# Expert weight places, routing order and token-ordered high and low rows in a transformer kernel

## The chip, the cores and the metric

The kernel runs on one core of a Trainium2 chip. The metric is the time of one execution in device microseconds, as the median of several runs.

## The reference, cut to what matters

A token batch of 256 rows of 1024 floats goes through two blocks of two layers each. The change touches only the mixture of experts in the two layers of the first block:

```python
def grouped_moe(h, router_w, router_bias, w_gate, w_up, w_down):
    xt = h.reshape(B * T, D)                      # T = 256 tokens, D = 1024
    aff = jax.nn.sigmoid((xt @ router_w).astype(jnp.float32))
    biased = aff + router_bias                    # 16 experts in 4 groups of 4
    # the group with the largest sum of its best two, then the best two experts in it
    gates = ...                                   # aff of the chosen two, divided by their sum
    hg = jnp.einsum('nd,edf->nef', xt, w_gate)    # 16 x 1024 x 512
    hu = jnp.einsum('nd,edf->nef', xt, w_up)      # 16 x 1024 x 512
    act = jax.nn.silu(hg) * hu * gates[:, :, None]
    return jnp.einsum('nef,efd->nd', act, w_down) # 16 x 512 x 1024
```

Ahead of it stand an attention mixer and a layer norm, behind it a second layer norm. All is fp32.

## The kernel before

Five instruction streams, one for each engine and one for SyncE (SP), are written by hand and meet through semaphores. `plan()` fixes beforehand in which PSUM bank each result lies (`job`) and in which SBUF slot of 8 KB per partition each piece of weights lies (`load`). SP issues the loads strictly in the order of the plan, each of 1 MB, and waits before each until the earlier user of the slot is done. A layer has 96 such loads for its experts, 12 for each of 8 pairs of experts (4 of gate, 4 of up, 4 of down). There are 18 slots: 0 to 5 are a ring, which also holds the mixer's weights and the output projection's (the last four, `wo0` to `wo3`); 6 to 11 are free once the output projection is done (`y11`); 12 to 17 lie under the attention's buffers and are free after the last head (`O15`). The list `places` says which slot each load takes: six of the ring, six of 12 to 17, six of 6 to 11, and again. In steady state a load goes to the slot of the load 18 before it.

The stages of a layer around the change are these.

- Norm, `norm` on VectorE (DVE) with `norm_and_transposed` on ScalarE (ACT): two tiles of 128 tokens (t = 0, 1), each `bn_stats`, the square root on ACT (`std_of`), and the writing of `x_tok`. TensorE (PE) transposes `x_tok` (L1802), ACT copies the transposes to `xT`, and PE multiplies them by the router's weights (L1807).
- High and low rows. The gather of tokens is a matmul with fp32r operands, so `x_tok` is split into `tok_high` (a copy rounded to fp32r, ACT) and `tok_low` (the rest, DVE, L1319). Both are written in a permuted order by `grouped`: expert weights are loaded with four consecutive rows of the matrix on one partition, so chunk c of 128 features holds every fourth one. ACT and DVE read `x_tok` through `spread`, with a step of four floats, and write consecutive floats.
- Routing, `route` on DVE: from `aff` (the sigmoid, ACT L903) to `chosen`, `gates`, `rank` (after four small products on PE) and `onehot` (L1304), a one-hot matrix of tokens by slots, 64 slots for each expert. `onehot` comes in two parts, for the first 4 experts and for the other 12, and each raises `slots_ready`.
- Gather, `tokens(j, n)` on PE (L1846): for four experts at a time, four results G{j}0 to G{j}3, each of two halves, each half the sum of four matmuls (high and low of both token tiles), with 128 columns of `tok_high` or `tok_low` stationary and 256 columns of `onehot` moving. ACT copies them to `xe`. j = 0 comes ahead of pair 0, j = 1 to 3 within pairs 1, 3 and 5.
- Pair p on PE: 64 matmuls of gate and up in four quarters (L1825), each quarter waiting for its two loads and freeing two slots behind it (`quarter_used`, `Hg`, `Hu`); the scatter of pair p-1 (L1857, L1858) from `y_high` and `y_low`; transposes of the hidden rows; 32 matmuls of down (L1835) into Y0 and Y1. DVE adds the scatter's results to `res` (L1327).
- `overflow`: rounds for experts with more than 64 tokens. The number of rounds is read from `rounds` into a register (L521) on each engine. With these inputs none is run.

## Time and profile before

| | |
|---|---|
| median of 3 runs | 1476.04 us (1474.61 to 1476.43) |
| the profiled execution | 1473.91 us |
| its span, first to last instruction | 1472.1 us |
| PE busy | 1340.2 us, 91% |
| DVE, ACT busy | 730.3 us, 522.2 us |
| expert stage of layer 0, from the first gate matmul to the last down matmul | 174.4 to 382.2 us |
| expert stage of layer 1 | 556.7 to 765.0 us |

The two expert stages are 28% of the span. The profile is of one execution; times in it are microseconds from the start of the span. 1.8 us of the profiled execution lie outside its span. PE's share of busy time is an average; between the norm and the first gate matmul PE is mostly idle, and within the expert stage it is nearly always busy.

### The profile page before, as it was taken

To read this page: it belongs to the slowest core of one execution; us is meant where nothing else is said; L and a number is where in the kernel's file an instruction comes from. 1 tells how busy PE (TensorE), PEld (TensorE's weight loads), DVE (VectorE), ACT (ScalarE), POOL (GpSimd) and SP (SyncE) were. 2 spreads that over 40 slices of the span, in tenths; PEclk is the share of its full clock that TensorE was granted. 3 is DMA by queue.
4 is the path that set the end of the run, shared out by engine and by line. 5 is a ranking of instruction groups with operands and counts; after the bars stand their busy time and mean duration, and the time that the engine had idled before them with its cause. 6 is when DMAs were issued, how large, how long until landed. Compare 5 with 4: busy or idle time off the path is not lost.

```text
span 1472.1 us, 19934 instructions
## 1 busy us (share of the span) xinstructions
PE 1340.2 (91%) x7792; PEld 964.1 (65%) x7792; DVE 730.3 (50%) x1387; ACT 522.2 (35%) x945; POOL 120.8 (8%) x135
## 2 busy tenths in 40 slices
PE   6999699998799879999978899789999888899997
PEld 3867543443376664444437888379998685699985
DVE  0656411211426661211125588587785636477766
ACT  1354321211123531211214323246654445276553
POOL 1012000000000300000002153030000002000000
PEclk9999799999899979999997999899999999999999
DMA  7252899999715288999996526755665440455740
GB/s 235 97 216 100 352 422 421 420 421 421 250 58 203 87 365 343 421 421 421 419 392 214 166 87 104 159 185 187 210 224 194 148 141 1 143 171 173 254 173 29
DMA packets 128050, 347.73 MB, mean 236 GB/s; under 512 B 8208, under 2 KB 84262, under 8 KB 103396
## 3 DMA queue, kind: packets, MB, share of 16 engines
q1 hardware_dynamic: 122576, 330.19, 59.7%
q0 software_dynamic: 4528, 15.84, 4.5%
q8 instruction: 53, 0.87, 0.2%
q10 hardware_dynamic: 868, 0.63, 0.2%
q14 instruction: 25, 0.20, 0.0%
HBM read 342.44 MB, written 4.19 MB: 235 GB/s over the span
## 4 chain that ended last, share of the span: by engine, by line
PE 82%; DVE 8%; DMA 4%; ACT 2%; issue 2%; POOL 0%; SPq 0%; DVEq 0%; ACTq 0%
PE bank L1825 14%; PE bank L1598 13%; PE bank L1964 8%; PE bank L1965 8%; PE bank L1966 8%; PE bank L1835 7%; DMA slot<-in_w_up 3%; PE bank L2085 2%; PE bank L1846 2%; PE bank L2089 2%; PE bank L2087 2%; PE bank L1999 2%; DVE ln_stats L1123 1%; DVE res L1128 1%; PE bank L1631 1%
## 5 line engine op out<-in xcount | busy, mean ns | idle before, releaser
L1964 PE MATMUL bank<-x_high,w_high 128*128 128x256 f32 x912 | 261.8, 287 | 0.0
L1965 PE MATMUL bank<-x_low,w_high 128*128 128x256 f32 x912 | 260.9, 286 | 0.0
L1966 PE MATMUL bank<-x_high,w_low 128*128 128x256 f32 x912 | 260.8, 286 | 0.0
L766 ACT ACTIVATE w_high<-slot 128x1024 fp32r<-128x1024 f32 x190 | 191.1, 1051 | 186.5 <-PE bank L1966 91.1
L1825 PE MATMUL bank<-slot,arena 128*64 128x512 f32 x1024 | 224.2, 593 | 11.8 <-DMA slot<-in_w_up 5.3
L1964 PEld LDWEIGHTS bank<-x_high,w_high 128*128 128x128 f32 x912 | 177.9, 195 | 1.8 <-issue 1.6
L1825 PEld LDWEIGHTS bank<-slot,arena 128*64 128x64 f32 x1024 | 76.2, 137 | 156.4 <-issue 156.4
L1965 PEld LDWEIGHTS bank<-x_low,w_high 128*128 128x128 f32 x912 | 177.8, 195 | 0.0
L1966 PEld LDWEIGHTS bank<-x_high,w_low 128*128 128x128 f32 x912 | 177.8, 195 | 0.0
L766 ACT ACTIVATE arena<-bank 128x512 f32<-128x512 f32 (+9 forms) x120 | 63.8, 540 | 226.1 <-PE bank L1882 86.7
L1495 DVE TENSOR_TENSOR w_low<-slot,w_high 128x1024 fp32r<-128x1024 f32 x88 | 103.8, 1222 | 59.8 <-ACT w_high L766 59.3
L1333 DVE TENSOR_TENSOR arena<-arena,bank 128x512 f32<-128x512 f32 x16 | 11.0, 689 | 216.8 <-PE bank L1825 216.8
L1835 PE MATMUL bank<-slot,arena 128*64 128x512 f32 x512 | 113.4, 596 | 1.1
L1341 DVE SCALAR_TENSOR_TENSOR y_low<-bank,slot_gates,y_high 128x512 fp32r<-128x512 f32 x32 | 24.0, 751 | 139.2 <-ACT y_high L925 138.4
L1598 PE MATMUL bank<-xT,slot 128*128 128x256 f32 x384 | 84.8, 381 | 0.0
L1598 PE MATMUL bank<-slot,arena 128*128 128x512 f32 (+1 forms) x192 | 80.5, 579 | 2.0 <-ACT arena L766 1.1
L1598 PEld LDWEIGHTS bank<-xT,slot 128*128 128x128 f32 x384 | 72.6, 190 | 11.6 <-issue 2.1
L1835 PEld LDWEIGHTS bank<-slot,arena 128*64 128x64 f32 x512 | 35.4, 137 | 66.2 <-issue 63.8
L1504 DVE TENSOR_TENSOR w_low<-slot,w_high 128x1024 fp32r<-128x1024 f32 x44 | 51.9, 1222 | 43.0 <-ACT w_high L766 42.8
L911 ACT ACTIVATE arena<-bank 128x512 f32<-128x512 f32 x16 | 9.6, 597 | 162.1 <-PE bank L1825 162.1
L1598 PEld LDWEIGHTS bank<-slot,arena 128*128 128x128 f32 x192 | 37.0, 195 | 42.9 <-issue 37.0
L693 POOL TENSOR_TENSOR arena<-arena,rinv 128x256 f32<-128x256 f32 (+1 forms) x48 | 38.6, 825 | 248.6 <-DVE rinv L1153 248.3
(284 smaller groups left out, 2070.4 us busy)
## 6 DMA issues: line engine op xcount, KB each, us to landing
slot<-in_w_gate SPq DMA_DIRECT2D x64, 1024.0 KB, 20.7
slot<-in_w_up SPq DMA_DIRECT2D x64, 1024.0 KB, 19.6
slot<-in_w_down SPq DMA_DIRECT2D x64, 1024.0 KB, 21.0
slot<-in_ffn_w_in SPq DMA_DIRECT2D x44, 1024.0 KB, 7.5
slot<-in_ffn_w_out SPq DMA_DIRECT2D x22, 1024.0 KB, 5.1
slot<-in_hgrn_w_in SPq DMA_DIRECT2D x16, 1024.0 KB, 6.8
slot<-in_w_in SPq DMA_DIRECT2D x10, 1024.0 KB, 8.8
slot<-in_w_o SPq DMA_DIRECT2D x8, 1024.0 KB, 5.0
```

The costliest lines, as they stand in the source:

```text
L693: ins = nc.gpsimd.tensor_tensor(w, w, by, ALU.mult)
L766: return nc.scalar.activation(dst, src, ACT.Copy)
L1495: V.tensor_tensor(w_low[c][:, ab, :, :], raw[:, :, P * c:P * (c + 1)], w_high[c][:, ab, :, :].bitcast(F32), ALU.subtract)\
L1504: V.tensor_tensor(flat(w_low[i % 2])[:, half], raw[:, half], flat(w_high[i % 2])[:, half].bitcast(F32), ALU.subtract).then_inc(sem("split" ...
L1598: last = mm(dst, lhs(c), rhs(c), start=(c == 0), stop=(c == n - 1))
L1825: last = mm(banks_gu["gu".index(m)][rows, :], xe[:, 4 * half + c, rows], ws[e][:, c, :], start=(half == 0 and c == 0), stop=(half == 1 and ...
L1835: last = mm(out[rows, :], B["actT"][:, c, rows], slot(W[(l, f"w{e}{c // 2}{names}")], 2, 1024)[:, c % 2, 512 * h:512 * (h + 1)], start=(c ...
L1846: last = mm(b[:, T * i:T * (i + 1)], x[:, t, tok(2 * n + i)], onehot[:, t, 4 * CAP * j:4 * CAP * (j + 1)], start=(k == 0), stop=(k == len( ...
L1964: mm(dst, high[:, k, :], x_high[:, k, :], start=(k == 0), stop=False)
L1965: mm(dst, high[:, k, :], x_low[:, k, :], start=False, stop=False)
L1966: last = mm(dst, low[:, k, :], x_high[:, k, :], start=False, stop=(k == KD - 1))
L1999: last = mm(b[:, tok(h)], k[:, 4 * s + h, tok(t)], q[:, 4 * s + h, tok(t)], start=True, stop=True)
```

## The change

1. `places` has a new pattern of 18: four of the ring, slots 12 to 17, two of the ring, slots 6 to 11. The last six loads of a layer lie in 12 to 17, as before.
2. ACT copies the second transposed half of token tile 0 before it takes the root for tile 1; it evaluates a sigmoid of one column right behind that root; it writes `tok_high` of tile 0 ahead of the router's sigmoid and of tile 1 behind it.
3. DVE writes `tok_low` of tile 0 behind `gates` and of tile 1 between the two parts of `onehot`, no longer ahead of the routing.
4. `tok_high` and `tok_low` are in token order, `grouped` is gone. ACT and DVE read and write consecutive floats, and PE's stationary operand is read through `spread`, 128 columns with a step of four floats (16 bytes). This holds for all 128 gather matmuls of a layer.
5. The first gather uses banks 0, 1, 5, 6 in place of 0, 1, 0, 1, and runs 12 matmuls that need no low rows of tile 1, then 4 with them, then the second halves. Pair p waits for G0 and G1 before its first quarter and for G2 and G3 before its third.
6. Down: the last two chunks are done by halves, so that Y0 is complete eight matmuls before Y1.
7. DVE reads `rounds` into a register before the last pair's additions.

ACT, layer 0, from the first root of the norm to the copies of the first gather (`arena<-bank`), before:

```order
L792 ACT_TABLE_LOAD
L792 ACTIVATE ln_std<-ln_mv,eps 128x1
L766 ACTIVATE xT<-bank 128x4x128
L792 ACTIVATE ln_std<-ln_mv,eps 128x1
L766 ACTIVATE xT<-bank 128x4x128 x3
L766 ACTIVATE tok_high<-x_tok 128x1024 x2
L903 ACT_TABLE_LOAD
L903 ACTIVATE aff<-bank 128x32
L766 ACTIVATE arena<-bank 128x512 x4
```

and after:

```order
L790 ACT_TABLE_LOAD
L790 ACTIVATE ln_std<-ln_mv,eps 128x1
L764 ACTIVATE xT<-bank 128x4x128 x2
L790 ACTIVATE ln_std<-ln_mv,eps 128x1
L809 ACT_TABLE_LOAD
L809 ACTIVATE loaded_table<-eps 128x1
L764 ACTIVATE xT<-bank 128x4x128 x2
L764 ACTIVATE tok_high<-x_tok 128x1024
L905 ACTIVATE aff<-bank 128x32
L764 ACTIVATE tok_high<-x_tok 128x1024
L764 ACTIVATE arena<-bank 128x512 x4
```

The table load and one of the two copies to `tok_high` stand ahead of the sigmoid `aff`, the other copy behind it.

DVE, layer 0, from the gates to the scaling of `res`, before:

```order
L1297 TENSOR_TENSOR gates<-gates,wsum 128x32 [waits dve_chain]
L1300 SCALAR_TENSOR_TENSOR rank<-bank1,chosen 128x32 [waits bank_full1,gates_ready]
L1301 TENSOR_REDUCE most<-bank1 128x1 [waits dve_chain]
L1304 TENSOR_TENSOR onehot<-rank,pos 128x256 x2
L1304 TENSOR_TENSOR onehot<-rank,pos 128x768 x2
```

and after:

```order
L1305 TENSOR_TENSOR gates<-gates,wsum 128x32 [waits dve_chain]
L1264 TENSOR_TENSOR tok_low<-x_tok,tok_high 128x1024 [waits tok_high,gates_ready]
L1309 SCALAR_TENSOR_TENSOR rank<-bank1,chosen 128x32 [waits bank_full1]
L1310 TENSOR_REDUCE most<-bank1 128x1 [waits dve_chain]
L1313 TENSOR_TENSOR onehot<-rank,pos 128x256 x2
L1264 TENSOR_TENSOR tok_low<-x_tok,tok_high 128x1024 [waits tok_high]
L1313 TENSOR_TENSOR onehot<-rank,pos 128x768 x2
```

Before, both `tok_low` stood directly ahead of the first step of the routing (`biased`), and each now follows where the row shows it.

DVE, layer 0, end of the last pair, before:

```order
L1327 TENSOR_TENSOR res<-res,bank5 128x512 [waits bank_full5]
L1327 TENSOR_TENSOR res<-res,bank6 128x512 [waits bank_full6]
L1327 TENSOR_TENSOR res<-res,bank3 128x512 [waits bank_full3]
L521 TENSOR_LOAD rounds [waits bank_free3,bank_free6,rounds_ready,bank_free5,bank_free7]
L521 ISA x2
L1350 COMPARE_AND_BRANCH
```

and after:

```order
L519 TENSOR_LOAD rounds [waits rounds_ready]
L519 ISA x2
L1332 TENSOR_TENSOR res<-res,bank7 128x512 [waits bank_full7]
L1332 TENSOR_TENSOR res<-res,bank5 128x512 [waits bank_full5]
L1332 TENSOR_TENSOR res<-res,bank6 128x512 [waits bank_full6]
L1332 TENSOR_TENSOR res<-res,bank3 128x512 [waits bank_full3]
L1356 COMPARE_AND_BRANCH [waits bank_free6,bank_free3,bank_free5,bank_free7]
```

The reading of the register stands ahead of the four additions instead of behind them.

The diff, cut to its lines with one line around each (lines that only hold "..." stand for what is left out):

```diff
         quarters = [(m, i) for i in range(2) for m in "gu"]
-        blocks = [(None, NSLOT, RAW_SLOTS)[n % 3] for n in range(12 * PAIRS // RAW_SLOTS - 1)] + [NSLOT]
-        places = [b if b is None else b + i for b in blocks for i in range(RAW_SLOTS)]
+        scratch, late = list(range(NSLOT, NSLOT + EXTRA)), list(range(RAW_SLOTS, NSLOT))
+        rounds = 12 * PAIRS // (NSLOT + EXTRA)
+        places = (4 * [None] + scratch + 2 * [None] + late) * rounds + scratch
...
         for n in range(4):
-            job(l, f"G0{n}", bank=n % 2)
+            job(l, f"G0{n}", bank=(0, 1, 5, 6)[n])
...
         eps = sb("eps", [P, 2])
+        loaded_table = sb("loaded_table", [P, 1])
...
             return tokens[:, t, :].rearrange("p (h q c) -> p h c q", h=2, c=4)
-        def grouped(tokens, t):
-            return tokens[:, t, :].rearrange("p (h c q) -> p h c q", h=2, c=4)
...
+            def high_rows(t):
+                copy(tok_high[:, t, :], x_tok[:, t, :]).then_inc(sem("tok_high"), 1)
...
                 half(0, 0)
+                half(0, 1)
                 std_of(2 * l, 1)
-                half(0, 1)
+                nc.scalar.activation(loaded_table[:, :], eps[:, 0:1], ACT.Sigmoid)
...
                 half(1, 1)
-                for t in range(NT):
-                    copy(grouped(tok_high, t), spread(x_tok, t)).then_inc(sem("tok_high"), 1)
+                act.wait_ge(sem("ln_done"), 4 * l + 2)
+                high_rows(0)
...
                 drained(nc.scalar.activation(aff[:, :, :], b[:, 0:NT * E].rearrange("p (t e) -> p t e", t=NT), ACT.Sigmoid), (l, "logit"))
+                high_rows(1)
...
+            def low_rows_of_tokens(l, t):
+                dve.wait_ge(sem("tok_high"), NT * l + t + 1)
+                V.tensor_tensor(tok_low[:, t, :], x_tok[:, t, :], tok_high[:, t, :].bitcast(F32), ALU.subtract).then_inc(sem("tok_low"), 1)
...
                 dve.wait_ge(sem("gates_ready"), l + 1)
+                low_rows_of_tokens(l, 0)
...
                     last.then_inc(sem("slots_ready"), 1)
+                    if first == 0:
+                        low_rows_of_tokens(l, 1)
...
                 link(V.tensor_scalar(res[:, :, :], x_tok[:, :, :], ALPHA, None, ALU.mult))
-            def low_rows_of_tokens(l):
-                for t in range(NT):
-                    dve.wait_ge(sem("tok_high"), NT * l + t + 1)
-                    V.tensor_tensor(grouped(tok_low, t), spread(x_tok, t), grouped(tok_high, t).bitcast(F32), ALU.subtract).then_inc(sem("tok_low"), 1)
...
                         drained(V.scalar_tensor_tensor(y_low[:, c], b[:, :], slot_gates[:, p:p + 1], y_high[:, c].bitcast(F32), ALU.mult, ALU.subtract), (l, f"Y{g}{p}"))
+                n_rounds = more_rounds(dve, l)
...
                         evacuated(dve, (l, f"M{t}{h}{PAIRS - 1}"))
-            def overflow(l):
-                n_rounds = more_rounds(dve, l)
+                return n_rounds
+            def overflow(l, n_rounds):
...
                 norm(2 * l, l, "y", True)
-                low_rows_of_tokens(l)
                 route(l)
-                experts(l)
-                overflow(l)
+                overflow(l, experts(l))
...
-            def down(l, outs, c, names):
-                for h, out in enumerate(outs):
+            def down(l, outs, c, names, halves=(0, 1)):
+                for h in halves:
+                    out = outs[h]
...
                         for k, (x, t) in enumerate(parts):
-                            last = mm(b[:, T * i:T * (i + 1)], x[:, t, tok(2 * n + i)], onehot[:, t, 4 * CAP * j:4 * CAP * (j + 1)],
+                            last = mm(b[:, T * i:T * (i + 1)], spread(x, t)[:, (2 * n + i) // 4, (2 * n + i) % 4, :], onehot[:, t, 4 * CAP * j:4 * CAP * (j + 1)],
...
                     done(last, (l, f"G{j}{n}"))
+                def first_tokens():
+                    bs = [reuse(pe, (l, f"G0{n}")) for n in range(4)]
+                    def parts(n, i, some):
+                        for x, t in some:
+                            last = mm(bs[n][:, T * i:T * (i + 1)], spread(x, t)[:, (2 * n + i) // 4, (2 * n + i) % 4, :], onehot[:, t, 0:4 * CAP],
+                                      start=(x is tok_high and t == 0), stop=(x is tok_low and t == 1))
+                        return last
+                    pe.wait_ge(sem("tok_high"), NT * (l + 1))
+                    pe.wait_ge(sem("tok_low"), NT * l + 1)
+                    pe.wait_ge(sem("slots_ready"), 2 * l + 1)
+                    begin, end = [(tok_high, 0), (tok_low, 0), (tok_high, 1)], [(tok_low, 1)]
+                    for n in range(4):
+                        parts(n, 0, begin)
+                    pe.wait_ge(sem("tok_low"), NT * (l + 1))
+                    for n in range(4):
+                        parts(n, 0, end)
+                    for n in range(4):
+                        done(parts(n, 1, begin + end), (l, f"G0{n}"))
...
                     if p % 2 == 0:
-                        for n in range(4):
+                        for n in range(2):
...
                             done(last, (l, ("Hg", "Hu")[q - 2] + str(p)))
+                        if q == 1 and p % 2 == 0:
+                            for n in range(2, 4):
+                                evacuated(pe, (l, f"G{p // 2}{n}"))
...
                     bs = [reuse(pe, (l, f"Y{h}{p}")) for h in range(2)]
-                    for c in range(MF):
-                        if c % 2 == 0:
-                            for e in range(2):
-                                loaded(pe, (l, f"w{e}{c // 2}{names}"))
+                    for e in range(2):
+                        loaded(pe, (l, f"w{e}0{names}"))
+                    for c in range(2):
                         for h, last in down(l, bs, c, names):
-                            if c == MF - 1:
-                                done(last, (l, f"Y{h}{p}"))
-                        if c == 1:
-                            last.then_inc(sem("rows_used"), 1)
-                pe.wait_ge(sem("tok_low"), NT * (l + 1))
-                pe.wait_ge(sem("slots_ready"), 2 * l + 1)
-                for n in range(4):
-                    tokens(0, n)
+                            pass
+                    last.then_inc(sem("rows_used"), 1)
+                    for e in range(2):
+                        loaded(pe, (l, f"w{e}1{names}"))
+                    for half in range(2):
+                        for c in range(2, MF):
+                            for h, last in down(l, bs, c, names, [half]):
+                                pass
+                        done(last, (l, f"Y{half}{p}"))
+                first_tokens()
...
                 scatter(PAIRS - 1)
```

## Rows read from the trace of the kernel before

**Rows 1.** The chain in order of time, layer 0, 154 to 175: start, us, what

```profile
154.33 1.91 ACT tok_high L766
...
156.27 3.48 DVE tok_low L1319 x2
...
160.07 0.20 DVE biased L1264
...
166.57 1.28 issue
167.85 5.57 PE bank L1846 x32
...
173.45 0.61 ACT arena L766
174.06 0.30 issue
```

**Rows 2.** Timelines, start, us, engine, line, operation [idle]: router to rank, both layers

```profile
153.72 3.18 PE L1807 MATMUL bank<-router,xT 128*128 128x16 f32 x16
...
158.17 1.28 ACT L903 ACT_TABLE_LOAD   x1
159.47 0.20 ACT L903 ACTIVATE aff<-bank 128x32 f32<-128x32 f32 x1
...
166.69 0.19 DVE L1300 SCALAR_TENSOR_TENSOR rank<-bank,chosen 128x32 f32<-128x32 f32 x1 [1.67 <-PE bank L1598]
...
535.91 3.60 PE L1807 MATMUL bank<-router,xT 128*128 128x16 f32 x16
...
542.45 0.20 DVE L1264 TENSOR_TENSOR biased<-aff,rbias 128x32 f32<-128x32 f32 x1
```

**Rows 3.** Groups by line and shape, 100 to 400: count, busy us, mean ns, idle

```profile
L766 ACT ACTIVATE w_high<-slot 128x1024 fp32r<-128x1024 f32 x4 | 4.2, 1060 | 7.6 <-PE bank L1659 7.6
L766 ACT ACTIVATE tok_high<-x_tok 128x1024 fp32r<-128x1024 f32 x2 | 3.9, 2014 | 0.0
...
L1166 DVE TENSOR_TENSOR w_low<-slot,w_high 128x1024 fp32r<-128x1024 f32 x4 | 4.9, 1226 | 7.6 <-ACT w_high L766 7.6
L1319 DVE TENSOR_TENSOR tok_low<-x_tok,tok_high 128x1024 fp32r<-128x1024 f32 x2 | 3.9, 1974 | 3.3 <-ACT tok_high L766 3.3
```

**Rows 4.** The chain at the second gather, in pair 1

```profile
213.86 3.78 PE bank L1846 x32
```

**Rows 5.** Stretches: busy us by engine, granted clock (1.00 is full), DMA share, GB/s

```profile
154.00:156.00 2.00, 2.00 (x13) 2.00 (x12) 0.00 (x0) 2.00 (x2) 0.00 (x0) 0.55 1.04 434
...
170.00:178.00 8.00, 7.05 (x42) 4.81 (x43) 1.27 (x2) 3.62 (x5) 0.00 (x0) 0.92 0.42 175
...
190.00:340.00 150.00, 149.65 (x759) 65.22 (x760) 24.72 (x37) 26.62 (x54) 1.12 (x2) 1.00 1.01 421
```

**Rows 6.** SP's queue of loads: start, us, operation

```profile
133.98 5.77 SPq L630 DMA_DIRECT2D slot<-in_w_gate  x2
...
178.04 0.81 SPq L630 DMA_DIRECT2D slot<-in_w_up  x2
```

**Rows 7.** PE's waits, 174.3 to 382.3: total us, times, longest

```profile
PE bank L1825 <- DMA slot<-in_w_up: 2.6, 2, 1.3
PE bank L1825 <- DMA slot<-in_w_gate: 2.2, 2, 1.3
```

**Rows 8.** End of the last pair, layer 0; L521: ns min/median/max, both layers

```profile
375.10 7.09 PE L1835 MATMUL bank<-slot,arena 128*64 128x512 f32 x32
...
381.43 1.49 ACT L925 ACTIVATE y_high<-bank,slot_gates 128x512 fp32r<-128x512 f32 x2 [5.68 <-PE bank L1835]
...
387.91 0.69 DVE L1123 BATCH_NORM_STATS2 ln_stats<-res 128x6 f32<-128x512 f32 x1 [1.37 <-issue]
...
L521 ACTq TENSOR_LOAD <-rounds x2: 290/383/476, 382.2 to 765.0; - x2
...
L521 DVEq TENSOR_LOAD <-rounds x2: 324/440/557, 386.8 to 769.6; - x2
```

## The prediction

> **What bounds the kernel now.** I read the chain of waits first, in order of time, and looked for where an expert stage starts and what holds it. The reader sees one path there: the copies to `tok_high` on ACT, the two `tok_low` on DVE, the routing on DVE from `biased`, 1.28 us of issue, the first gather of 5.57 us, ACT's last copy and another 0.30 us, and then the first gate matmul at 174.36 [rows 1]. So the high and low rows stand in the path of the routing, though the routing needs nothing of them. Next came the timelines of ACT and PE at that place: the router's products on PE are over at 153.72 + 3.18 = 156.90, but ACT takes the sigmoid at 159.47, behind its two copies and a table load of 1.28 us [rows 2].
>
> Then the DMA. SP can refill a slot only when PE has used it; the first such load of layer 0 goes out at 178.04 [rows 6]. Before that the queues run dry: 42% of 170 to 178 is 3.4 us, so the first 18 loads are in at about 173.4. From 190 on the stage moves 421 GB/s without a gap [rows 5]. 78 loads of 1.049 MB and 2.1 MB of norm rows at 421 GB/s are 199.3 us, from 178.04 to 377.3. PE's last 32 down matmuls run from 375.10 to 382.2 [rows 8], and the second half of them, from about 378.6, needs the last weights. PE itself has only 4.8 us of waits for weights in the whole stage, all in pair 7 [rows 7]. So both the transfers and PE's work hang on the moment when pair 0 starts; the transfers bind, and PE is 4.8 us behind them. Layer 1's stage takes as long, 208.3 us against 207.8.
>
> **The change part by part.** Sums go against the profiled execution (1473.91 us, span 1472.1) and are then taken off the median, 1476.04, which is 2.1 us above it.
>
> *Routing ahead of the high and low rows.* ACT: the table load moves into the idle time ahead of the last two transposes' copies, `tok_high` of tile 0 becomes a copy from consecutive to consecutive floats. Such a copy of 128x1024 is there: 1060 ns for `w_high`, against 2014 ns now [rows 3]. It starts at 154.33 and is done at 155.4, before the router's 156.90. The sigmoid (0.20 us [rows 2]) then follows the router, and `biased` starts at about 157.15, not 160.07 [rows 1]: 2.9 us. In layer 1 the router ends at 535.91 + 3.60 = 539.51 and `biased` can start at 539.75, not 542.45 [rows 2]: 2.7 us. What was removed from this path is queued again where nothing is late: `tok_high` of tile 1 (1.06 us) runs on ACT beside 5 us of routing; `tok_low` of tile 0 takes 1226 ns, as `w_low` does [rows 3], in the 1.67 us in which DVE waits for PE's rank products [rows 2]. `tok_low` of tile 1 stands behind the first part of `onehot` and is ready about 1.3 us after the gather starts; 12 of its 32 matmuls, at 5.57/32 us each or more [rows 1], are 2.1 us, so the gather does not wait. The second part of `onehot` is 1.2 us later and is used in pair 0's last third. These come out at nothing; without the cover, `tok_low` would cost 1.2 us in each layer.
>
> The clock: PE's was at 0.55 of full in 154 to 156 and comes back late in the first gather [rows 5]. PE now does tile 0's router products 1.2 us earlier and idles later, so the clock may fall up to 1.2 us sooner; work in that time would take twice as long. Bounds 0 and 0.6 us in layer 0, none in layer 1, where it has fallen by then; I take 0.3.
>
> *The first gather's banks.* The last matmul ends at 173.42 and the first gate matmul starts at 174.36, after the copy of G3 and 0.30 us [rows 1]. Afterwards G0 to G3 are complete 4 matmuls apart (0.47 us at full clock), pair 0 needs G0 and G1 alone, and their copies (0.61 us each) end 0.2 us before the gather does. Pair 0 starts 0.1 us behind it: 0.8 us in each layer.
>
> *Places of the loads.* Six loads go out behind `O15`, near 126, and no longer behind 133.98 and the output projection's weights [rows 6]. The first 18 loads are in at about 163 instead of 173.4. That alone gains nothing, since the refill starts with pair 0. It sees to it that a pair 0 that starts earlier finds its weights and that the queues are free. In steady state every load still follows the one 18 before it. The last six now follow the ones 14 before, not 12, with the queues still full then: nothing.
>
> *Down by halves.* Y0 is ready some 0.9 us sooner, ACT's two `y_high` (1.49 us back to back [rows 8]) are no longer back to back, and Y1's can start 0.3 us earlier. DVE's second `y_low` follows. I take 0.2 us in each layer, in the last pair; elsewhere the next pair's gate and up hide it. Bounds 0 and 0.7.
>
> *The register.* DVE idles 1.37 us between the last addition and the next norm, with the reading of `rounds` in it (440 ns and two steps more) [rows 8]. Put ahead of the additions, it runs on the sequencer beside `y_low`: ACT's sequencer does the same at 382.2, when its engine is still at `y_high` [rows 8]. What is left is the wait for the last addition and a branch, some 0.45 us. 0.9 us in each layer; if the reading held the engine up, it would be 0.
>
> *The stride.* This is the open term. 128 stationary loads in each layer now read 128 columns 16 bytes apart. No operation of PE in this trace does. From below: a gather of 32 matmuls takes 3.78 us, 0.118 us each [rows 4], set by 256 moving columns, and the load runs beside them; if it stays under 0.118 us, the cost is nothing. From above: ACT's copy with the same step takes 2014 ns and not 1060, DVE's 1974 and not 1226 [rows 3]. ACT's strided column costs up to 1.83 ns; 128 of them are 0.235 us, twice the pace of a matmul now. I take the lower end: the loads have a path of their own beside the moving columns, and those already take four columns (16 bytes) in 4 x 0.118/256 = 1.85 ns, so the row nearest to it in kind, PE's own, shows no limit yet. It is a choice and not a reading.
>
> The Trainium skill, "SBUF — State Buffer", section "Door 1: The DMA port swizzle", speaks against it: full bandwidth needs at least two accesses in a line of 16 bytes, which this step never has. ACT's and DVE's rows agree with that. By it the sum would be that of rival 2 below.
>
> **Sum.** Layer 0: 2.9 - 0.3 + 0.8 + 0.2 + 0.9 = 4.5. Layer 1: 2.7 + 0.8 + 0.2 + 0.9 = 4.6. Together 9.1 us: 1476.0 - 9.1 = **1466.9 us** (1464.8 for a run like the profiled one). The transfers and PE both move with pair 0, so the stage passes all of it on.
>
> **Rivals.** 1 (forecast): the stride costs nothing or less than 0.02 us a load; 1464.5 to 1470.
>
> 2, slower: the stationary load becomes the bound in the gathers. At 0.235 us a matmul the first gather takes 7.5 us, not 5.57: +2.0. The other three take 96 x 0.117 = 11.2 us more, of which pair 7's waits absorb 4.8: +6.4. Two layers: +16.8 - 9.1 = +7.7, **1483.7 us**. It decides where 128 loads take the layer's 5.57 + 3 x 3.78 us of gathers, 4.8 us of slack and 4.6 us of gain, 26.3 us in all: a load above 0.205 us makes the kernel slower. For it: ACT and DVE, two engines, both show the cost. Against it: PE's moving columns.
>
> 3, between: a load of some 0.18 us. The first gather 5.8 us, +0.2; the others 6.0 - 4.8 = +1.2; two layers +2.8: **1469.7 us** (1467 to 1475).
>
> 4, the change does not do what it says: the earlier pair 0 is not passed on, because the transfers, not the slots, bind from the start. Then only the ends of the stages gain, 2.2 us: **1473.8 us**. Against it: the queues are 58% idle between 170 and 178 [rows 5].
>
> **How the numbers follow.** Chances: 1 0.55, 2 0.28, 3 0.12, 4 0.05. A measurement here can tell about 0.2%, 2.95 us, from no change. Faster: nearly all of 1, three quarters of 3, part of 4: 0.65. Same: the rest of 3 and 4 and the mild end of 2 (a load of 0.21 to 0.22 us): 0.12. Slower: 0.23. The range of 8 in 10 takes in 1, 3 and 4 and the nearer half of 2: 1464.5 to 1484.5. The likeliest case's own range is 1464.5 to 1470.
>
> **What would show it.** In the profile after: `biased` at about 157.2; the first gather from about 165 with matmuls still 0.118 us apart at full clock; the first refill at about 174.5; DMA at 421 GB/s from then on; pair 7 still waiting some 4.8 us for weights; layer 0's last down matmul at about 378.5; 0.5 us in place of 1.37 before the norm. The gathers at 213.86 and its fellows are where the stride shows: 3.78 us if I am right, 7.5 if rival 2 is, and then pair 7 waits for nothing. I am wrong also if the clock falls before the transposes of tile 1, or if DVE's first `tok_low` ends after the rank products.

## The result, and the profile after

The changed kernel takes **1481.03 us** (median of 6 runs, 1480.18 to 1483.38) where the kernel before takes 1476.14 (6 runs beside it, 1473.93 to 1477.43): a ratio of 1.0041 with a 95% interval of 1.003 to 1.0052. It is slower by 4.9 us, and the forecast was 9.1 us faster. It is rival 2 that came true, with 1483.7 us in its sum: the stationary columns 16 bytes apart became the bound in the gathers. The time lies inside the range only because the range took in the nearer half of that rival; the forecast's own case ended at 1470 us. The profiled execution took 1481.08 us with a span of 1479.3, against 1473.91 and 1472.1.

The groups of PE's weight loads in layer 0's gathers, by line and shape from 176 to 400 us (count, busy us, mean ns); the records of the kernel before have 188 and 189 ns for the same loads. Behind them the groups of the copies, 150 to 172 us:

```profile
L1851 PEld LDWEIGHTS bank<-onehot,tok_low 128*128 128x128 f32 x48 | 15.9, 331 | 0.0
L1851 PEld LDWEIGHTS bank<-onehot,tok_high 128*128 128x128 f32 x48 | 15.8, 330 | 0.0
...
L1264 DVE TENSOR_TENSOR tok_low<-x_tok,tok_high 128x1024 fp32r<-128x1024 f32 x2 | 2.4, 1222 | 0.0
L764 ACT ACTIVATE tok_high<-x_tok 128x1024 fp32r<-128x1024 f32 x2 | 2.1, 1048 | 0.0
```

In these rows `PEld` is PE's weight load, which runs beside its matmuls (`PE`); the last two numbers of a row are busy us and the mean ns of one. ACT and DVE got what was forecast: 1048 and 1222 ns in place of the 2014 and 1974 of [rows 3]. The same step in memory, taken off them, now lies on PE. The chain has the second gather, and PE's timeline shows its pace, start to start:

```profile
213.12 7.53 PE bank L1851 x32
```

```profile
213.20 0.40 PE L1851 MATMUL bank<-onehot,tok_low 128*128 128x256 f32 x1
213.44 0.40 PE L1851 MATMUL bank<-onehot,tok_high 128*128 128x256 f32 x1
```

7.53 us in place of 3.78 [rows 4]; 0.235 us a matmul and not 0.118. Nothing waits for anything here, and PE is recorded as busy: a load that takes longer than its neighbour's moving columns shows only as pace.

The chain where layer 0's stage starts, to be held against [rows 1]:

```profile
151.56 0.76 DVE x_tok L1136
...
152.36 1.97 PE bank L1806 x8
154.33 3.44 PE bank L1811 x16
157.77 0.02 issue
157.79 0.21 ACT aff L905
...
158.12 0.20 DVE biased L1272
...
165.75 0.14 issue
165.88 7.78 PE bank L1861 x32
173.66 2.72 PE bank L1829 x11
```

The copies are gone from the path, and the gate matmuls stand right behind the gather. The 1.28 us of issue is no saving: it was the time of DVE's `rank`, `most` and first `onehot` (from 166.69, 166.91 and 167.00 in DVE's timeline before), and the chain now shows these three by name, 1.23 us from the end of the rank products to the gather. From `biased` to the gather it is 7.8 us in both kernels. But `biased` starts at 158.12 and not at 157.15, the gather takes 7.78 us and not 5.57, and pair 0 starts at 173.59, only 0.77 us sooner than before. The granted clock tells of the first of these (columns: busy us of PE, PEld, DVE, ACT, POOL, then clock, DMA share, GB/s):

```profile
150.00:152.00 2.00, 0.98 (x9) 0.88 (x8) 1.89 (x4) 1.78 (x3) 0.00 (x0) 0.78 0.99 418
152.00:154.00 2.00, 1.64 (x8) 1.57 (x8) 0.97 (x2) 0.49 (x1) 0.00 (x0) 0.50 1.01 422
...
168.00:170.00 2.00, 2.00 (x10) 2.00 (x10) 1.90 (x6) 0.00 (x0) 0.00 (x0) 0.50 0.00 0
170.00:172.00 2.00, 2.00 (x10) 2.00 (x10) 0.38 (x1) 0.75 (x2) 0.00 (x0) 0.60 0.00 0
190.00:340.00 150.00, 149.77 (x706) 72.36 (x703) 24.22 (x37) 25.30 (x51) 1.12 (x2) 1.00 1.01 421
```

The shares of these stretches put PE at the upper level (2.4 GHz) until about 151.1 and at the lower (1.2 GHz) until about 171.6; before, it was at the lower from about 154.2 to 171.3 [rows 5]. So the last transposes and the router's products all ran at half clock. The transfers are as they were, 421 GB/s.

PE's waits from 172 to 390 us no longer have the two lines of [rows 7]. The largest that are left:

```profile
PE bank L1884 <- DVE y_low L1346: 1.0, 1, 1.0
PE bank L1912 <- DVE arena L1338: 0.9, 1, 0.9
```

and the end of the last pair, to be held against [rows 8]:

```profile
386.07 0.75 DVE L1346 SCALAR_TENSOR_TENSOR y_low<-bank,slot_gates,y_high 128x512 fp32r<-128x512 f32 x1 [6.26 <-ACT y_high L928]
387.73 0.75 DVE L1346 SCALAR_TENSOR_TENSOR y_low<-bank,slot_gates,y_high 128x512 fp32r<-128x512 f32 x1 [0.91 <-ACT y_high L928]
...
391.61 1.29 DVE L1126 BATCH_NORM_STATS2 ln_stats<-res 128x6 f32<-128x512 f32 x2 [0.37 <-DVE res L1332]
```

0.37 us of idle time, no longer 1.37: the register's microsecond is there.

**Stretches that leave the drift out.** Two profiles of the same instructions differ by up to 1.8 us where layer 0's first norm starts and by some 3 us in the part behind the second stage, in which nothing was changed. So I read three points in each profile: the first `BATCH_NORM_STATS2` of layer 0's norm, the first behind layer 0's stage, the first behind layer 1's. Each profile is of one execution, and that need not be a typical one: the profiled execution of the kernel before is 2.2 us under its median, that of the changed kernel on it, that of `e3_pairs` 3.5 under and that of `f3_pairs_busy` 2.8 over. The differences between the points, in us:

| kernel | norm to norm, layer 0 | layer 1 | both, less before |
|---|---|---|---|
| before | 246.04 | 382.87 | 0 |
| changed | 249.76 | 385.74 | +6.6 |
| e1_grouped | 243.56 | 379.66 | −5.7 |
| e2_stride_only | 252.43 | 388.19 | +11.7 |
| e3_pairs | 242.53 | 379.54 | −6.8 |
| e4_eights | 250.57 | 386.39 | +8.1 |
| f1_before_pairs | 244.47 | 381.56 | −2.9 |
| f2_pairs_old_places | 242.59 | 379.59 | −6.7 |
| f3_pairs_busy | 238.93 | 377.21 | −12.8 |
| f4_plain_rows | 253.54 | 391.93 | +16.6 |
| g1_stride_busy | 247.26 | 383.27 | +1.6 |
| g2_more_busy | 238.03 | 375.90 | −15.0 |
| g3_old_tail | 242.07 | 379.30 | −7.5 |

### The profile page after: what moved, and what is told of

The parts are those of the page before. It is cut to its first block, busy times and chain, and to the rows that moved or that the text cites. A ratio compares the mean times of both kernels' runs of the same rounds, so it can differ in the third digit from the quotient of the medians.

```text
span 1479.3 us, 19931 instructions
## 1 busy us (share of the span) xinstructions
PE 1366.0 (92%) x7792; PEld 988.7 (67%) x7792; DVE 727.4 (49%) x1387; ACT 519.2 (35%) x947; POOL 120.9 (8%) x135
## 4 chain that ended last, share of the span: by engine, by line
PE 87%; DVE 8%; ACT 2%; issue 2%; DMA 1%; POOL 0%; SPq 0%; DVEq 0%; ACTq 0%
PE bank L1829 15%; PE bank L1602 13%; PE bank L1840 8%; PE bank L1995 8%; PE bank L1996 8%; PE bank L1997 8%; PE bank L1851 3%; PE bank L2116 2%; PE bank L2118 2%; PE bank L2120 2%; PE bank L2030 2%; DVE res L1131 1%; DVE ln_stats L1126 1%; PE bank L1635 1%; PE bank L1884 1%
## 5 line engine op out<-in xcount | busy, mean ns | idle before, releaser
L1499 DVE TENSOR_TENSOR w_low<-slot,w_high 128x1024 fp32r<-128x1024 f32 x88 | 103.8, 1222 | 59.5 <-ACT w_high L764 59.1
L1508 DVE TENSOR_TENSOR w_low<-slot,w_high 128x1024 fp32r<-128x1024 f32 x44 | 51.9, 1222 | 43.0 <-ACT w_high L764 43.0
```

The source lines that it names most:

```text
L1499: V.tensor_tensor(w_low[c][:, ab, :, :], raw[:, :, P * c:P * (c + 1)], w_high[c][:, ab, :, :].bitcast(F32), ALU.subtract)\
L1508: V.tensor_tensor(flat(w_low[i % 2])[:, half], raw[:, half], flat(w_high[i % 2])[:, half].bitcast(F32), ALU.subtract).then_inc(sem("split" ...
```

## The experiments

The theory after the result (A): the step of 16 bytes costs 0.117 us in each of 256 stationary loads, and the rest of the change is a gain. Its rivals were that the gathers' slowness comes with something else of the package (order, banks), and that any step would do it. The kernel before, run beside each batch, took 1475.38, 1475.19 and 1476.02 us.

### The package without the step, and the step without the package

Everything of the change but its stationary columns, which lie grouped again as before:

```diff
-copy(tok_high[:, t, :], x_tok[:, t, :]).then_inc(sem("tok_high"), 1)
+copy(grouped(tok_high, t), spread(x_tok, t)).then_inc(sem("tok_high"), 1)
...
-last = mm(..., spread(x, t)[:, (2 * n + i) // 4, (2 * n + i) % 4, :], ...)
+last = mm(..., x[:, t, tok(2 * n + i)], ...)
```

> The changed kernel with the high and low rows back in the permuted order: PE's stationary columns are consecutive, ACT and DVE read with a step of 16 bytes again; all the rest of the change stays. Theory A (the strided stationary load is the whole loss): gathers of 32 matmuls back to 3.78 us (0.118 us each), the first gate matmul at about 172.0, pair 7 waits for weights again; about 7.4 us under the kernel before, 1468.7 us. Theory B (the new order of routing, places and first gather costs what it was meant to gain): 1476 us or more, with the gathers at 3.78 us all the same.

Measured: 1470.15 us (1469.08 to 1471.97), ratio 0.9963 [0.995, 0.9977]. That is 5.2 us under the kernel before beside it, where theory A gave 7.4. The chain has the first gather and the second:

```profile
166.77 6.57 PE bank L1865 x32
...
212.78 3.77 PE bank L1855 x32
```

The other way round, the kernel before with rows in token order and the strided gather, and nothing else:

```diff
-copy(grouped(tok_high, t), spread(x_tok, t)).then_inc(sem("tok_high"), 1)
+copy(tok_high[:, t, :], x_tok[:, t, :]).then_inc(sem("tok_high"), 1)
...
-last = mm(..., x[:, t, tok(2 * n + i)], ...)
+last = mm(..., spread(x, t)[:, (2 * n + i) // 4, (2 * n + i) % 4, :], ...)
```

> The kernel before with the token order and the strided stationary columns alone; order of routing, places, banks, down and register as before. Theory A: `biased` 2.1 us sooner since both copies are cheaper, first gather 7.8 us instead of 5.6, the other three 7.53 instead of 3.78, of which pair 7's waits absorb 5.7 us: +5.65 us in each layer, 1487.4 us. Theory B (the stride is not the loss): only the cheaper copies count, 1472 us or less.

Measured: 1488.4 us (1487.1 to 1490.14), ratio 1.009 [1.0074, 1.0105], 1.0 us over what theory A gave; its second gather:

```profile
214.67 7.53 PE bank L1846 x32
```

The two agree. The step takes the gather from 3.77 to 7.53 us with and without the package. Between the medians of the changed kernel and `e1_grouped` it costs 10.9 us of time, and 10.1 when each is held against the kernel before beside it. The package alone gains 5.2 us, though the slower copies are back and one of them, `tok_low` of tile 0 with 2.0 us, stands in its chain ahead of `rank`.

### Which step

Token rows in which the four chunks of a half lie as two pairs: stationary columns are 8 bytes apart, and the copies read and write by twos.

```diff
+def paired(tokens, t, h):
+    return tokens[:, t, 512 * h:512 * (h + 1)].rearrange("p (a q b) -> p a q b", a=2, b=2)
+def in_pairs(tokens, t, h):
+    return tokens[:, t, 512 * h:512 * (h + 1)].rearrange("p (q a b) -> p a q b", a=2, b=2)
...
+last = copy(paired(tok_high, t, h), in_pairs(x_tok, t, h))
...
+last = mm(..., paired(x, t, k // 4)[:, k % 4 // 2, :, k % 2], ...)
```

> The changed kernel with the high and low rows stored so that a stationary column follows the last by 8 bytes (two of them in 16 bytes), and ACT and DVE read and write pairs of consecutive floats, in two instructions for each copy. Theory A1 (a load is slow when each column lies in another 16 bytes): matmuls 0.118 us apart, ACT's copies about 1.2 us together, 1468.3 us. Theory A2 (any step but one float doubles the load): matmuls 0.235 us apart, 1481 us.

Measured: 1469.92 us (1466.45 to 1471.19), ratio 0.996 [0.9947, 0.9974]. The load and the gather:

```profile
L1867 PEld LDWEIGHTS bank<-onehot,tok_low 128*128 128x128 f32 x48 | 9.5, 197 | 0.0
L1867 PEld LDWEIGHTS bank<-onehot,tok_high 128*128 128x128 f32 x48 | 9.4, 196 | 0.0
...
210.75 3.86 PE bank L1867 x32
```

The medians of `e3_pairs` and `e1_grouped` are 0.2 us apart, which tells nothing. From the last `x_tok` of layer 0's norm to the first gate matmul it is 20.21 us against 21.14.

And 32 bytes, with all eight chunks interleaved:

```diff
-last = mm(..., spread(x, t)[:, (2 * n + i) // 4, (2 * n + i) % 4, :], ...)
+last = mm(..., eights(x, t)[:, (2 * n + i) // 4, :, (2 * n + i) % 4], ...)
```

> The changed kernel with a stationary column following the last by 32 bytes. Theory A1 (one access for each 16 bytes touched): matmuls 0.235 us apart as with 16 bytes, 1481 us. Rival (the cost grows with the step): 0.47 us apart, gathers of 15 us, some 1535 us. If the step of 8 and of 32 bytes both give 0.235, the step as such is what costs.

One execution, 1485.43 us:

```profile
L1859 PEld LDWEIGHTS bank<-onehot,tok_low 128*128 128x128 f32 x48 | 16.2, 338 | 0.0
...
213.89 7.73 PE bank L1859 x32
```

It is 4.4 us over the changed kernel, with stretches 1.5 us longer. So the load's time is not in proportion to the step: 188, 197, 330 and 338 ns for 4, 8, 16 and 32 bytes, or 0.118, 0.12, 0.235 and 0.242 us a matmul. The edge lies between 8 and 16 bytes. The Trainium skill, "SBUF — State Buffer", section "Door 1: The DMA port swizzle", asks for at least two accesses in a line of 16 bytes. By that rule 8 bytes are free and 16 are not, and this case agrees with it. The four steps fit the rule but do not prove the line: a step of 12 bytes was not run. The same section of the Trainium skill counts a step of four fp32 as free; here that step is the one that doubles the load, and the measurement decides.

### Where the package's gain is, and the places

The kernel before with the layout in pairs and nothing else, in its old order:

```diff
-copy(grouped(tok_high, t), spread(x_tok, t))
+for h in range(2):
+    last = copy(paired(tok_high, t, h), in_pairs(x_tok, t, h))
...
-last = mm(..., x[:, t, tok(2 * n + i)], ...)
+last = mm(..., chunk(x, t, 2 * n + i), ...)
```

`chunk` picks the columns 8 bytes apart, as in `e3_pairs`.

> The kernel before with one thing changed: the high and low rows are stored so that a stationary column follows the last by 8 bytes and ACT and DVE move pairs of floats. Order of routing, places, banks, down and register as before. Theory A (the rows' layout costs the copies 2.0 us each and the routing waits for them; a step of 8 bytes is free for PE): `biased` about 1.8 us sooner in each layer, gathers 0.12 us a matmul, 1472.5 us. Rival (the layout brings nothing without the new order, since DVE waits for the table load): within 1 us of the kernel before.

Measured: 1474.84 us (1473.3 to 1476.38), ratio 0.9998 [0.9989, 1.0008]. ACT's timeline at the router:

```profile
156.17 2.34 ACT L774 ACTIVATE tok_high<-x_tok 128x512 fp32r<-128x512 f32 x4
158.53 1.28 ACT L913 ACT_TABLE_LOAD   x1
159.82 0.20 ACT L913 ACTIVATE aff<-bank 128x32 f32<-128x32 f32 x1
```

The shorter copies alone don't help much: the table load still stands between them and the sigmoid. The stretches say 2.9 us less, the time 0.4. So the gain of `e3_pairs`, 5.5 us of time and 6.8 in the stretches, comes for the most part from the rest of the package (order, places, banks, down, register), of which only the places and the register were run by themselves.

`e3_pairs` with the places of the kernel before:

```diff
-places = (4 * [None] + scratch + 2 * [None] + late) * rounds + scratch
+places = [b if b is None else b + i for b in blocks for i in range(RAW_SLOTS)]
```

> The changed kernel with the 8-byte layout, and the places of the loads as in the kernel before. Theory A (the places only bring the first 18 loads in earlier, and the refill starts with pair 0): within 1 us of the 8-byte kernel, 1469.5 us, with the first 18 loads in at about 172. Rival (pair 0 starts so early that the transfers still run, or a slot binds at the end): 2 us or more slower than that.

Measured: 1469.53 us (1466.92 to 1471.31), ratio 0.9965 [0.9954, 0.9977], the same. The stretch 163 to 180 with the old places and, in the second fence, with the new:

```profile
163.00:180.00 17.00, 15.75 (x76) 10.12 (x77) 6.11 (x14) 3.56 (x5) 0.00 (x0) 0.76 0.82 330
```

```profile
163.00:180.00 17.00, 15.75 (x76) 9.84 (x78) 5.76 (x14) 3.56 (x5) 0.00 (x0) 0.78 0.28 108
```

The initial loads move from 163 to 180 to before 163, and no matmul starts sooner for it.

### The clock

What was still open was why `e3_pairs` gains 5.5 us and not the 9.1 of the sum. Theory C: PE idles around the routing, its clock falls, and what the change starts sooner it also starts at half clock. So PE is given, in `e3_pairs`, 10 transposes of the identity matrix behind tile 0's router products, 30 behind tile 1's and 8 behind the rank products, into a bank that nobody reads then:

```diff
+def busy(n):
+    for _ in range(n):
+        nc.tensor.transpose(bank[4][:, 0:P], ident[:, :], ident[:, :])
...
+busy(10)   # after the router's products of tile 0
...
+busy(30)   # after those of tile 1
...
+busy(8)    # after the rank products
```

> The changed kernel with the 8-byte layout, and 10, 30 and 8 transposes of the identity into an unused bank, behind the router's products of tile 0, behind those of tile 1 and behind the rank products: work whose result nobody reads, in time in which PE waits. Theory C (PE's clock falls in the idle time around the routing and stays low into the first gather): clock 1.00 throughout, router of tile 1 in 1.9 us and not 3.3, rank products 1.2 and not 2.3, first gather 3.9 and not 6.7; about 5 us in each layer, 1459.5 us. Rival (the clock falls all the same): 30 transposes at 0.22 us outlast the 4.6 us of waiting by 2 us, and the kernel is 4 us slower than the 8-byte kernel, 1473.5 us.

Measured: 1461.4 us (1459.06 to 1464.17), ratio 0.9902 [0.9885, 0.9919]. PE's timeline in layer 0, and the first gathers of layers 0 and 1 in the chain and the timeline:

```profile
154.05 1.96 PE L1832 MATMUL bank<-router,xT 128*128 128x16 f32 x16
155.86 3.47 PE L1820 MATMUL bank<-ident 128*128 128x128 f32 x30
160.60 0.37 PE L1840 MATMUL bank<-chosen,tables 128*128 128x16 f32 x2 [1.27 <-DVE chosen L1315]
```

```profile
163.78 4.72 PE bank L1886 x32
```

The router's products take 1.96 us where they took 3.44, the gather 4.72. The clock was not at 1.00 throughout, as theory C had it: in layer 0 it fell during the 8 transposes, at 161.8, and was back at 165.2. In layer 1 it fell behind the same 1.2 us of idle time and its first gather took 6.45. The four executions lie in two pairs, 1459.1 and 1459.5 us with a mean granted clock of 0.972, and 1463.4 and 1464.2 with 0.968; the median lies between the pairs and the profile is of the longest. The next kernel fills that time: 40 and 12 transposes for 30 and 8.

```diff
-busy(30)
+busy(40)
...
-busy(8)
+busy(12)
```

> As f3_pairs_busy (8-byte step), with 40 transposes of the identity matrix behind the router's products in place of 30, and 12 behind the rank products in place of 8. It asks whether the first gather of layer 1, which still took 6.45 us at the lower clock in f3_pairs_busy against 4.72 in layer 0, can be kept at the upper clock. Ten more transposes at 0.11 us fill 1.1 of the 1.2 us in which PE still waited for the chosen experts. Theory E (what remains of the low clock follows that idle time): the rank products stay at the upper clock in both layers, layer 1's first gather falls to 4 to 4.8 us and layer 0's to 3.9 to 4.7; pair 0 starts 1.5 to 2.5 us sooner in layer 1 and up to 0.8 us in layer 0: 1461.4 - 2.5 = 1459 us. Rival (the clock falls at the same place although PE is no longer idle there, and the 12 transposes at half speed end after onehot is ready): the same or up to 1.5 us slower, 1461.4 to 1463.

Measured: 1460.06 us (1459.74 to 1460.99), ratio 0.9895 [0.988, 0.991]; the chain has the first gathers of layer 0 and of layer 1, and the stretch around layer 0's routing is at full clock throughout:

```profile
163.45 4.10 PE bank L1886 x32
...
538.50 3.99 PE bank L1886 x32
```

```profile
156.00:166.00 10.00, 9.26 (x81) 8.85 (x80) 9.33 (x40) 1.06 (x2) 0.00 (x0) 1.00 0.85 355
```

Theory E holds in both gathers, and the four executions now lie within 1.3 us. In layer 1 the clock still fell at the end of the router's products and into the 40 transposes (0.60 from 530 to 534), but it was back before the rank products. There the transposes cost something too: `chosen` was done at 534.5, and the rank products started behind the last transpose, at 535.96. In layer 0 the rank products are over so early that `tok_low` of tile 0 stands in the chain ahead of `rank`; its cover is used up. This is the fastest kernel of the study, 16.0 us ahead of the kernel before. From the last `x_tok` of the norm to the first gate matmul, layer 0 has 22.79 us before, 22.03 changed, 20.21 in `e3_pairs` and 15.91 here.

The same transposes in the changed kernel, with its step of 16 bytes:

```diff
 last = mm(..., spread(x, t)[:, (2 * n + i) // 4, (2 * n + i) % 4, :], ...)
...
+busy(10)
...
+busy(30)
...
+busy(8)
```

> The changed kernel, its 16-byte step in the stationary columns kept, with the same 10 + 30 + 8 transposes of the identity matrix put into PE's idle time around the routing as in f3_pairs_busy. It asks whether the price of the step depends on PE's clock. Theory D (the stationary load reads at a pace of its own, 0.235 us for 128 columns, at both clock levels): the first gather stays at 7.5 to 7.8 us although the clock is at its upper level for most of it, and the transposes gain only what the router's and rank products win, some 2.5 to 3 us in each layer against the changed kernel, not the 4 to 5 us of f3_pairs_busy: 1481.0 - 5.5 = 1475.5 us (1474 to 1477). Rival (the step's price scales with PE's clock, so that the first gather at full clock falls well below 7.5 us, or the gain is that of f3_pairs_busy against e3_pairs, 8.5 us): 1472.5 us or less.

Measured: 1478.22 us (1476.42 to 1479.62), ratio 1.0013 [1.0004, 1.0022]. Around the first gather, stretches of PE alone (busy us, clock, DMA share, GB/s) and the chain:

```profile
164.00:166.00 2.00, 1.52 (x7) 1.00 0.66 274
166.00:168.00 2.00, 2.00 (x10) 0.73 0.04 16
168.00:170.00 2.00, 2.00 (x10) 0.50 0.00 0
```

```profile
164.48 7.80 PE bank L1870 x32
```

PE's timeline in that gather at 0.50, and in the second fence the first gather of the kernel before, with consecutive columns, at 0.50 too; then the load records of the first gathers of `e1_grouped` (least, median, largest ns), consecutive as well:

```profile
168.38 0.44 PE L1870 MATMUL bank<-onehot,tok_high 128*128 128x256 f32 x1
168.62 0.44 PE L1870 MATMUL bank<-onehot,tok_low 128*128 128x256 f32 x1
```

```profile
169.06 0.42 PE L1846 MATMUL bank<-onehot,tok_low 128*128 128x256 f32 x1
169.28 0.41 PE L1846 MATMUL bank<-onehot,tok_high 128*128 128x256 f32 x1
```

```profile
L1865 PEld LDWEIGHTS bank<-onehot,tok_high x32: 187/330/331, 166.7 to 551.8; 128*128 128x128 f32 x32
```

With the step the matmuls start 0.235 us apart at 1.00 and 0.238 at 0.50, and all 32 take 7.80 us: the strided load hardly sees PE's clock. Consecutive columns do: 0.118 us at 1.00 and 0.214 at 0.50, and their load goes from 187 ns to 330, which is what the strided load has at both levels. So the step costs 0.117 us a matmul at 1.00 and only 0.024 at 0.50, where matmuls with consecutive columns need 0.214 as well. The rival, whose time was 1472.5 or less, is out. Theory D's mechanism holds and its time does not: it gave 1475.5 us (1474 to 1477), a gain of 5.5, and the gain is 2.8. The way from norm to pair 0 is 2.5 us shorter in each layer, as it said, and the stretches show 5.0, but this time doesn't show all of it.

### Plain rows

If the gate and up weights were loaded so that nothing need be permuted (row 128k + p on partition p), the step would not be needed at all, but each transfer is then cut into pieces of 2 KB:

```diff
-if is_expert(name):
+if is_expert(name) and name[1][0] == "w":
     return src
...
-last = mm(..., spread(x, t)[:, (2 * n + i) // 4, (2 * n + i) % 4, :], ...)
+last = mm(..., x[:, t, tok(2 * n + i)], ...)
```

> The changed kernel with nothing permuted: gate and up weights are loaded with row 128 k + p on partition p, in pieces of 2 KB and not 8 KB, the high and low rows stay in token order, the stationary columns are consecutive. Theory A (the stride is the loss, the transfers do not mind the piece): gathers 0.118 us a matmul, 421 GB/s, 1469 us. Rival (pieces of 2 KB are slower): under 421 GB/s from 190 on, and each per cent of that costs some 2 us in each layer.

Measured: 1490.83 us (1490.75 to 1492.44), ratio 1.0107 [1.009, 1.0123]; the stretch in steady state, and PE's waits in layer 0's stage:

```profile
190.00:340.00 150.00, 143.06 (x722) 62.62 (x718) 24.69 (x37) 24.86 (x49) 1.12 (x2) 1.00 1.04 397
```

```profile
PE bank L1829 <- DMA slot<-in_w_up: 9.2, 5, 2.4
PE bank L1829 <- DMA slot<-in_w_gate: 6.3, 4, 1.8
```

397 GB/s in place of 421 over transfers that bind the stage: the permuted rows are paid for by the transfers, and giving them up costs more than the step did. The gathers are quick again (3.79 us the second), so the loss lies with the transfers.

### The register

`e3_pairs` with the register read behind the last additions again:

```diff
-n_rounds = more_rounds(dve, l)
 add(PAIRS - 1)
...
+n_rounds = more_rounds(dve, l)
 with dve.If(n_rounds > 0):
```

> e3_pairs with one part of the change undone: DVE's reading of the number of rounds into a register stands behind the last additions again, not ahead of them. It measures the register's term by itself. Theory F (the change's register edit is worth 0.9 to 1.0 us at the end of each layer's expert stage, as the 0.37 us against 1.37 us before bn_stats say, and nothing takes it back): 1469.9 + 1.9 = 1471.8 us, and 1.37 us of idle time ahead of the first bn_stats again. Rival (most of it is given back in the mixer of layer 1 or at the end of the program, where something else is late): within 0.5 us of e3_pairs, 1469.9 to 1470.4.

Measured: 1470.41 us (1467.21 to 1471.32), ratio 0.9966 [0.9952, 0.9979], 0.5 us over the median of `e3_pairs`, and 0.15 us better than it when each is held against the kernel before beside it. That is the rival's time and not theory F's 1471.8. The place itself is clear:

```profile
383.94 1.29 DVE L1140 BATCH_NORM_STATS2 ln_stats<-res 128x6 f32<-128x512 f32 x2 [1.36 <-issue]
```

1.36 us again, against 0.36 in `e3_pairs` (1.45 against 0.70 in layer 1): 1.75 us in sum. Yet the stretches of this profile are 0.7 us shorter than those of `e3_pairs`, since in layer 0 the clock came back at 168.0 and not at 170.6, and the first gather took 5.44 us in place of 6.72, with the same instructions. So the register's term is shown at its place and not in the time; the moment of the clock's return moves more than it is worth.

## Why the prediction was wrong

**The step that failed** is the last part edit by edit, *the stride*, with "I take the lower end". I had both ends, 0.118 and 0.235 us, and the price came out at the upper one. That it agrees to three digits is luck: the 1.83 ns a column behind it is in no row, ACT's 2014 ns over 1024 columns are 1.97 and DVE's 1974 are 1.93, which would give 0.25 us. The row I leaned on, PE's moving columns at 1.85 ns for 16 bytes, reads consecutive floats; that it passes four of them in 1.85 ns says how fast PE takes a line, not that it can take a line for each column. Read that way it points at the upper end: 128 columns in 128 lines at 1.85 ns are 0.237 us. ACT's row and DVE's row were two engines' direct evidence of this step, against one row of another pattern. `e1_grouped` and `e2_stride_only` show that the stride alone reverses the sign, and `e3_pairs` that a step of 8 bytes would not have.

**Rival 2's sum** against the profile, by stage: it has +8.4 − 4.5 = +3.9 in layer 0 and +3.8 in layer 1; the stretches have +3.7 and +2.9. Its threshold, a load above 0.205 us, held, with the load at 0.235. The 3 later gathers cost 3 x 3.75 = 11.25 us as worked out. From the start of pair 6's down matmuls to pair 7's were 345.38 to 375.10 before, with the waits for weights inside, and 355.79 to 379.80 now: 5.7 us were absorbed, not 4.8, so each of the four stops cost some 0.2 us more than the wait in the list.

**Routing order.** Layer 1 was right: `biased` at 543.52, of which 3.74 is the later norm (`x_tok` at 533.31 and 537.05), is 539.78; forecast 539.75. Layer 0 gained 1.95 us and not 2.9 − 0.3.

**The clock** was a second term that came out wrong. I set it to 0.3 us, bounds 0 and 0.6, in layer 0 alone. It came out at 1.0 us there before `biased`, since the clock fell before tile 1's transposes and not after them, which the prediction had named as a way to be wrong. And a second cost was missing: the clock came back at 171.3 before and 171.6 after, though the gather began 2 us sooner, and so that gather spends 2 us more at half clock. Counted from the last `x_tok` it came back after 19.6 to 20.4 us in both layers of the kernel before, the changed kernel, `e1_grouped` and `e3_pairs`; `g3_old_tail`, with 16.4 and 17.2, shows that this is no constant. In `e3_pairs` it takes 6.72 us where 5.57 was in the sum; in the changed kernel this is hidden, since the step makes it 7.78 us at either clock. From the last `x_tok` to pair 0, `e3_pairs` wins 2.6 and 2.5 us in the two layers, forecast 3.4 and 3.5; that is 1.8 of the 3.0 us by which its 1469.9 misses the 1466.9. `f3_pairs_busy` and `g2_more_busy` show the cause: with PE kept at work, the way from the last `x_tok` to pair 0 is shorter than before by 6.3 and 5.2 us in the first and by 6.9 in each layer in the second.

**The first gather's banks**: 0.94 us of idle time ahead of the gate matmuls before, 0 after; forecast 0.8. **Cover for the copies**: both `tok_low` ran where the sum had put them, at no cost. **The places**: nothing, as forecast (`f2_pairs_old_places`). **The register**: 1.0 and 0.75 us at its place, forecast 0.9. **Down by halves**: forecast 0.2, got 0. The second `y_low` ends 1.6 us behind the end of the down matmuls in both kernels (383.77 and 382.19 before, 388.48 and 386.89 after): ACT's two `y_high` back to back were already done 0.7 us behind the matmuls, as Y1's alone is now.

**What stays open.** The stretches of the changed kernel are 6.6 us longer and its median 4.9. Most of that is the choice of execution: the two profiled ones are 7.2 us apart, since that of the kernel before is 2.2 under its median. For `f1_before_pairs` the stretches are 2.9 shorter and the profiled executions only 0.6; there the difference lies outside the stretches, 1.3 us ahead of layer 0's norm and 1.0 behind layer 1's, where nothing was changed. How much of each median is the moment of the clock's fall and return, one profile each does not settle. And in layer 1's +2.9 about 0.5 us have no row.

## What to carry to other kernels

A permutation is paid by the copies, by the stationary operand or by the transfers; split between copies and operand with 8 bytes for a step, it cost next to nothing here. Before moving a stride from a copy to a matmul's stationary operand, count its columns per 16 bytes, and hold the load's time against the pace of the matmul beside it, because a load that is too slow shows as no wait at all. Give a fast path's evidence to the access pattern it was measured with, and to no other. A stage that is started sooner may start at a lower clock: look at the granted clock across the idle time ahead of it. If PE waits there for another engine, transposes of the identity matrix that nobody reads can be worth more than the reordering itself, as long as they do not outlast the wait by more than they win.

## What the runs showed of the hardware

- A stationary load of 128 columns of 4 bytes takes 188 ns with columns 4 bytes apart, 197 at 8, 330 at 16 and 338 at 32, by its records at the upper clock; back to back with 256 moving columns that is a pace of 0.118, 0.12, 0.235 and 0.242 us.
- At 16 bytes the pace is 0.235 us at the upper level of PE's clock and 0.238 at the lower; with consecutive columns it is 0.118 and 0.214, and the load's record 188 and 330 ns.
- ACT's copy of 128x1024 takes 1048 ns between consecutive rows, and 2 x 648 with groups of two floats, against 2014 with a step of 16 bytes; DVE's subtraction 1222, 2 x 687 and 1974.
- 48 more transposes in each layer whose result nobody reads made the kernel 8.5 us faster, and 62 in each 9.9 us (1469.9, 1461.4 and 1460.1 us).
- Loads of a megabyte in pieces of 2 KB ran at 397 GB/s, in the longer pieces of the changed kernel at 421.
